# Down projection of a MoE's expert blocks: three rounded products of high and low parts in place of one full-precision product

## The chip, the cores and the metric

The kernel runs on one core of a Trainium2 chip. The time is device microseconds (us) of one execution; a result is the median of several runs. The profile is of one execution, with its own time beside it. Engine names: PE is TensorE, ACT is ScalarE, DVE is VectorE, POOL is GpSimd, SP is SyncE, which here only issues transfers.

## The reference, cut to what matters

One layer of a diffusion backbone: a mixer (mLSTM and RG-LRU), then a mixture of experts over 1152 tokens of width 1024 (64 experts of width 256, eight per token, one shared expert), then a final norm. The change touches one product, the last one of `expert_block`:

```
def expert_block(args):
    tok, e = args
    xb = x2d[tok]                                  # 128 gathered tokens x 1024
    hb = jax.nn.silu(xb @ exp_w1[e]) * (xb @ exp_w3[e])   # 128 x 256
    return hb @ exp_w2[e]                          # 256 -> 1024
yb = lax.map(expert_block, (slot_tok.reshape(NB, MOE_BLOCK), block_expert))
routed = segment_sum(yb.reshape(P, D) * slot_w[:, None], slot_tok, num_segments=N)
```

All arithmetic of the reference is float32.

## The kernel before, in words

The stages run one after the other, a barrier between them: norm, RG-LRU, mLSTM, routing, experts, final norm. The change is wholly in `stage_experts` (line 1350). Routing leaves a list of blocks of 128 token slots, each of one expert; the shared expert is taken as expert 64 with nine blocks at the end of the list. In this execution there are 114 blocks. Each engine has its own loop over pairs of blocks (Fori, two blocks in an iteration); the order of work on an engine is written out by hand and is fixed, and engines meet only through counting semaphores. An instruction that waits holds up all that is behind it on its engine.

What each engine does for block b, in the order of its loop:

- PE (lines 1574 to 1579): `turn_h(b)` transposes the 128x256 hidden tile (two transposes); `up(b+1)` computes both up projections of the next block; `turn(b+2)` transposes the gathered tokens of the block after (eight transposes); `down(b)` is the down projection: two halves of 512 columns, two steps of 128 along the inner width, four float32 matmuls, each of which the trace shows as two PE records. `up` already works as the change makes `down` work: its two operands are kept as a high part, rounded to the format fp32r, and a low part, the rest, and high*high + high*low + low*high is summed, 24 matmuls a block.
- ACT (lines 1622 to 1628): `ht(b)` copies the transposed hidden tile to SBUF; `high(b+2)` writes the rounded high part of the up weights, two instructions of 128x2048; `silu(b+1)`; `xt(b+2)` copies the transposed tokens, rounding them, two instructions; `y_half(b)` copies the result of `down(b)` from PSUM, two instructions (lines 1603 and 1604), after waiting that `down(b)` is done and that POOL has raised `scatter_done` for this buffer.
- DVE (lines 1667 to 1671): `low(b+2)` subtracts the high part from the up weights, two instructions of 128x2048 with both inputs in SBUF; `hidden(b+1)` multiplies silu, gate and slot weight; `x_low(b+2)` subtracts the high part of the tokens, two instructions that read PSUM.
- POOL (lines 1518 to 1521): `gather(b+4)` copies an index column and issues the gather of 128 rows; `scatter(b)` waits until the scatter before has landed (line 1503 then raises `scatter_done`), copies an index column, waits for `y_half(b)`, and issues a scatter that adds 128 rows of 1024 to the result in DRAM.
- SP (lines 1464 to 1469): the weights of an expert are three transfers of 1 MB in three slots: `issue_up` (lines 1414 and 1415) waits until the last block of the expert three before has its low part, `issue_down` (line 1424) waits for `down_done` of such a block.

Buffers: tokens, up-weight parts and y have two each; the PSUM tile of `down` and the transposed hidden tile have one.

Of the kernel before, what the change touches and what calls it, by code (L numbers as in the profile page):

```python
# [10 lines left out]
F32 = mybir.dt.float32  # L11
BF16 = mybir.dt.bfloat16
F32R = mybir.dt.float32r
# [1336 lines left out]
def stage_experts(nc, a, m):  # L1350

    with ExitStack() as ctx:
# [7 lines left out]
        wup = [[sb(f"wup{part}{j}", [P, 2, KT, DE], F32R) for part in "hl"] for j in range(2)]  # L1360
        idx_g, idx_s = [sb(f"idx_g{j}", [P, 1], I32) for j in range(2)], sb("idx_s", [P, 1], I32)
        hs, hb = [sb(f"hs{j}", [P, DE]) for j in range(2)], [sb(f"hb{j}", [P, DE]) for j in range(2)]
        hT = sb("hT5", [P, 2, P])
        y = [sb(f"y{j}", [P, D]) for j in range(2)]
        b_turn, b_up, b_h, b_down = m.banks[1:3], m.banks[3:5], m.banks[5], m.banks[6:8]
        s_w, s_w2 = [sem(f"ld_w{j}") for j in range(WSLOT)], [sem(f"ld_w2_{j}") for j in range(WSLOT)]
# [6 lines left out]
        w1 = a["exp_w1"][0].rearrange("e (p k) n -> e p k n", k=KT)  # L1373
        w3 = a["exp_w3"][0].rearrange("e (p k) n -> e p k n", k=KT)
        wd = a["exp_w2"][0].rearrange("e (p j) n -> e p j n", j=2)
        w_high, w_low, xt_low = (sem(n) for n in ("w_high", "w_low", "xT_low"))
        HALVES = [slice(0, 1), slice(1, 2)]
        block = ctx.enter_context(nc.Block())

# [5 lines left out]
        def pairs(eng):  # L1385
            return eng.value_load(m.tab[0:1, 4 * P + NE:4 * P + NE + 1], min_val=1, max_val=TABLE // 2)
# [7 lines left out]
        def expert(eng, b):  # L1394

            return entry(eng, bass.ds(b, 1), NE)
# [5 lines left out]
        @block.sync  # L1402
        def _(sp):
            def up_weights(e, r=None):

                slot = e % WSLOT
                if r is not None:
                    x = bass.ds(r * WSLOT + e, 1)
                    p1, p3 = (w[x].rearrange("e p k n -> (e p) k n") for w in (w1, w3))
                elif e < NE:  # L1410
                    p1, p3 = w1[e], w3[e]
                else:
                    p1, p3 = (a[n][0].rearrange("(p k) n -> p k n", k=KT) for n in ("shared_w1", "shared_w3"))
                sp.dma_start(w13[:, slot, 0, :, :], p1).then_inc(s_w[slot], 16)
                sp.dma_start(w13[:, slot, 1, :, :], p3).then_inc(s_w[slot], 16)

            def down_weights(e, r=None):
                if r is not None:
                    p2 = wd[bass.ds(r * WSLOT + e, 1)].rearrange("e p j n -> (e p) j n")
                elif e < NE:  # L1420
                    p2 = wd[e]
                else:
                    p2 = a["shared_w2"][0].rearrange("(p j) n -> p j n", j=2)
                sp.dma_start(w2[:, e % WSLOT, :, :], p2).then_inc(s_w2[e % WSLOT], 16)

            def ends(e, r=None):

                at = 4 * P + e
                return entry(sp, slice(at, at + 1) if r is None else bass.ds(r * WSLOT + at, 1), TABLE, 1)

            def issue_up(e, r=None):

                sp.wait_ge(w_low, 2 * ends(e - WSLOT, r))
                up_weights(e, r)

            def issue_down(e, r=None):

                sp.wait_ge(down_done, ends(e - WSLOT, r))
                down_weights(e, r)

            def up_landed(e, n):
                sp.wait_ge(s_w[e % WSLOT], 32 * n)
                sp.sem_inc(w_ready, 1)  # L1443

            def down_landed(e, n):
                sp.wait_ge(s_w2[e % WSLOT], 16 * n)
                sp.sem_inc(w2_ready, 1)

            up_weights(0)
            for e in range(1, WSLOT):  # L1450
                up_weights(e)
                down_weights(e - 1)
            down_weights(WSLOT - 1)
            up_landed(0, 1)
            down_landed(0, 1)
            up_landed(1, 1)
            for e in range(WSLOT, 2 * WSLOT):
                issue_up(e)
                up_landed(e - 1, (e - 1) // WSLOT + 1)
                if e > WSLOT:  # L1460
                    issue_down(e - 1)
                down_landed(e - 2, (e - 2) // WSLOT + 1)
            FULL = NE // WSLOT
            with sp.Fori(2, FULL) as r:
                for e in range(WSLOT):
                    issue_up(e, r)
                    up_landed(e - 1, r + (1 if e >= 1 else 0))
                    issue_down(e - 1, r)
                    down_landed(e - 2, r + (1 if e >= 2 else 0))
            for e in range(FULL * WSLOT, NX):  # L1470
                issue_up(e)
                up_landed(e - 1, (e - 1) // WSLOT + 1)
                issue_down(e - 1)
                down_landed(e - 2, (e - 2) // WSLOT + 1)
            up_landed(NE, NE // WSLOT + 1)
            issue_down(NE)
            for e in range(NE - 1, NX):
                down_landed(e, e // WSLOT + 1)
# [48 lines left out]
        def _(pe):  # L1527
# [25 lines left out]
                    mm = pe.transpose(b_h[:, i * P:(i + 1) * P], hb[j][:, i:DE:2], m.ident)  # L1553
                mm.then_inc(ht_out, 1)

            def down(b, j):
                e = expert(pe, b)
                slot = e % WSLOT
                pe.wait_ge(w2_ready, e + 1)
                pe.wait_ge(ht_ready, b + 1)  # L1560
                pe.wait_ge(y_act, b + 1)
                for half in range(2):
                    for i in range(2):
                        mm = pe.matmul(b_down[half][:, :], hT[:, i, :],  # L1564
                                       w2[:, bass.ds(slot, 1), i, half * 512:(half + 1) * 512].rearrange("p s n -> p (s n)"),
                                       start=(i == 0), stop=(i == 1))
                mm.then_inc(down_done, 1)

            n = pairs(pe)
# [4 lines left out]
            with pe.Fori(0, n) as r:  # L1574
                for u in range(2):
                    turn_h(r * 2 + u, u)
                    up(r * 2 + (u + 1), 1 - u)
                    turn(r * 2 + (u + 2), u)
                    down(r * 2 + u, u)

        @block.scalar
        def _(act):
# [12 lines left out]

            def ht(b):
                act.wait_ge(ht_out, b + 2)
                act.activation(hT[:, :, :], b_h[:, 0:DE].rearrange("p (i n) -> p i n", i=2), ACT.Copy).then_inc(ht_ready, 1)

            def y_half(b, j):  # L1600
                act.wait_ge(down_done, b + 1)
# [4 lines left out]
            def high(b, j):  # L1606
# [5 lines left out]
                for half in HALVES:  # L1612
                    act.activation(part13(wup[j][0], half), raw13(e % WSLOT, half), ACT.Copy).then_inc(w_high, 1)  # L1613

            n = pairs(act)
            act.sem_inc(y_act, 1)
            high(0, 0)
# [1 line left out]
            xt(1, 1)  # L1619
            high(1, 1)  # L1620
            silu(0, 0)
            with act.Fori(0, n) as r:
                for u in range(2):
                    ht(r * 2 + u)
                    high(r * 2 + (u + 2), u)
                    silu(r * 2 + (u + 1), 1 - u)
                    xt(r * 2 + (u + 2), u)
                    y_half(r * 2 + u, u)

        @block.vector  # L1630
        def _(dve):
            def hidden(b, j):
                dve.wait_ge(act_done, b + 1)
                if not (isinstance(b, int) and b < 2):
                    dve.wait_ge(ht_out, b)
                weight = m.slots[:, bass.ds(column(dve, b), 1), 1:2].rearrange("p c w -> p (c w)").bitcast(F32)
                dve.scalar_tensor_tensor(hb[j][:, :], hs[j][:, :], weight, b_up[j][:, DE:2 * DE], ALU.mult, ALU.mult).then_inc(h_done, 1)

            def low(b, j):

                e = expert(dve, b)
                dve.wait_ge(w_ready, e + 1)
                if not (isinstance(b, int) and b < 2):
                    dve.wait_ge(up_done, b - 1)
                for i, half in enumerate(HALVES):
                    dve.wait_ge(w_high, 2 * b + (i + 1))
                    dve.tensor_tensor(part13(wup[j][1], half), raw13(e % WSLOT, half),  # L1647
                                      part13(wup[j][0], half).bitcast(F32), ALU.subtract).then_inc(w_low, 1)

            def x_low(b, j):  # L1650

                dve.wait_ge(xt_ready, b + 1)
                if not (isinstance(b, int) and b < 2):
                    dve.wait_ge(up_done, b - 1)
                for i in range(2):
                    ins = dve.tensor_tensor(xT[j][1][:, 4 * i:4 * i + 4, :], b_turn[i][:, :].rearrange("p (k n) -> p k n", k=4),  # L1656
                                            xT[j][0][:, 4 * i:4 * i + 4, :].bitcast(F32), ALU.subtract)
                ins.then_inc(xt_low, 1)

            dve.sem_inc(h_done, 1)  # L1660
            low(0, 0)
            x_low(0, 0)
            x_low(1, 1)
            low(1, 1)
            hidden(0, 0)
            n = pairs(dve)
            with dve.Fori(0, n) as r:
                for u in range(2):
                    low(r * 2 + (u + 2), u)
                    hidden(r * 2 + (u + 1), 1 - u)  # L1670
                    x_low(r * 2 + (u + 2), u)


def stage_final(nc, a, o, m):
# [133 lines left out]
```

## Time and profile before

| | us |
|---|---|
| median of 3 runs | 2596.17 (2587.87 to 2598.42) |
| profiled execution, its own time | 2599.9 |
| its span in the trace | 2598.1 |
| start of the first y copy of `y_half` (block 0) | 1287.3 |
| start of the last one (block 113) | 2503.3 |

The span of the trace is the time from its first to its last instruction; the execution's own time has 1.8 us around it. The expert stage is read by its y copies: one per block, 113 intervals in 1216.0 us.

### The profile page before, as it was taken

What the parts mean: (1) busy time and instruction counts of PE and PEld (TensorE: products, weight loads), DVE (VectorE), ACT (ScalarE), POOL (GpSimd) and SP (SyncE); (2) the same over time, 40 slices, a digit from 0 to 9 for tenths busy, and PEclk for the clock granted to TensorE, in tenths of its full rate; (3) what the DMA queues carried; (4) which work ended last, traced back from release to release, by engine and by line L of the source; (5) the groups of instructions that cost most, each with busy time, mean ns of one, the idle gap of its engine ahead of it and who ended that gap; (6) DMA issues with size and microseconds to landing.
All of it is one profiled execution on the core that took longest, in us unless ns stands there. A gap on an engine that the chain in (4) does not pass through costs nothing. (4 is left out here: it accounts for less than half of the span.)

```text
span 2598.1 us, 30671 instructions
## 1 busy us (share of the span) xinstructions
PE 2072.1 (80%) x8111; PEld 1365.7 (53%) x8112; DVE 1290.0 (50%) x2151; ACT 1015.9 (39%) x1496; POOL 689.1 (27%) x616
## 2 busy tenths in 40 slices
PE   5587477499976785992599999999999989999950
PEld 0143233254866673541376666666766666666730
DVE  1334534500044554787365555556555555555547
ACT  1133434300011221110366555556665555555631
POOL 3010000000000000255134444444443444445430
PEclk9798687799977887995799999999999999999985
DMA  9741000021010004420797898976788899997554
GB/s 281 229 146 35 1 16 0 10 64 33 17 25 1 1 1 150 179 82 25 272 337 198 282 317 259 303 234 177 231 256 281 268 301 298 310 286 237 111 148 170
DMA packets 118319, 426.57 MB, mean 164 GB/s; under 512 B 22396, under 2 KB 36732, under 8 KB 93308
## 3 DMA queue, kind: packets, MB, share of 16 engines
q1 hardware_dynamic: 71372, 279.86, 29.4%
q0 software_dynamic: 46512, 145.97, 22.9%
q8 instruction: 27, 0.44, 0.1%
q14 instruction: 24, 0.20, 0.0%
q10 hardware_dynamic: 384, 0.11, 0.0%
HBM read 340.79 MB, written 85.67 MB: 164 GB/s over the span
## 5 line engine op out<-in xcount | busy, mean ns | idle before, releaser
L1647 DVE TENSOR_TENSOR wupl<-w,wuph 128x2048 fp32r<-128x2048 f32 x232 | 521.5, 2289 | 546.9 <-ACT wuph L1613 539.8
L1613 ACT ACTIVATE wuph<-w 128x2048 fp32r x232 | 432.3, 1918 | 38.3 <-SPq L1443 37.2
L1564 PE MATMUL bank<-w,hT 128*128 x912 | 415.7, 599 | 2.0 <-issue 1.7
L1546 PE MATMUL bank<-wuph,xTh 128*128 128x512 f32 x920 | 370.2, 402 | 17.7 <-DVE xTl L1656 17.7
L1546 PE MATMUL bank<-wuph,xTl 128*128 128x512 f32 x920 | 361.9, 393 | 0.0
L1546 PE MATMUL bank<-wupl,xTh 128*128 128x512 f32 x920 | 361.0, 392 | 0.0
L1564 PEld LDWEIGHTS bank<-w,hT 128*128 128x128 f32 x912 | 165.4, 191 | 172.3 <-issue 171.9
L1498 POOL DMA_INDIRECT xg<-hn_scratch,idx_g x118 | 211.2, 1790 | 96.3 <-POOL idx_g L1490 93.4
L1506 POOL DMA_INDIRECT yacc_scratch<-y,idx_s x114 | 184.1, 1615 | 115.6 <-ACT y L1604 65.7
L1603 ACT ACTIVATE y<-bank 128x512 f32<-128x512 f32 x114 | 68.2, 598 | 360.9 <-POOLq L1503 198.5
L1546 PEld LDWEIGHTS bank<-wuph,xTh 128*128 128x128 f32 x920 | 174.7, 190 | 55.6 <-issue 21.7
L1546 PEld LDWEIGHTS bank<-wuph,xTl 128*128 128x128 f32 x920 | 173.5, 189 | 37.1
L1546 PEld LDWEIGHTS bank<-wupl,xTh 128*128 128x128 f32 x920 | 174.1, 189 | 33.7
L1533 PE MATMUL bank<-cst,xg 128*128 128x128 f32 x928 | 127.8, 282 | 72.6 <-DMA xg<-hn_scratch,idx_g 69.9
L1490 POOL COPY idx_g<-shared 128x1 int32 x118 | 166.9, 1414 | 50.4 <-PE bank L1533 34.8
L1490 POOL COPY idx_s<-shared 128x1 int32 x114 | 51.5, 452 | 450.9 <-DMA yacc_scratch<-y,idx_s 444.3
L1533 PEld LDWEIGHTS bank<-cst,xg 128*128 128x128 f32 x928 | 121.1, 193 | 92.6 <-DMA xg<-hn_scratch,idx_g 85.7
L1656 DVE TENSOR_TENSOR xTl<-bank,xTh 128x512 fp32r<-128x512 f32 x232 | 148.8, 683 | 16.1 <-ACT xTh L1588 16.0
L864 PE MATMUL bank<-hnT,wg 128*128 128x512 f32 (+1 forms) x384 | 128.2, 497 | 33.1 <-DMA wg<-in_w_in 32.2
L1157 PE MATMUL bank<-wo,yT 128*128 128x512 f32 x288 | 130.2, 612 | 14.5 <-DMA wo<-in_w_out 14.5
L485 PE MATMUL bank<-hnT,wg 128*128 128x512 f32 (+1 forms) x384 | 131.6, 507 | 12.3 <-DMA bd<-in_rg_wx 12.2
L993 DVE SCALAR_TENSOR_TENSOR eb<-bank,cols,cst 128x128 f32<-128x128 f32 x72 | 20.3, 345 | 228.7 <-PE bank L898 228.4
(311 smaller groups left out, 2489.1 us busy)
## 6 DMA issues: line engine op xcount, KB each, us to landing
w<-in_exp_w SPq DMA_DIRECT2D x192, 1024.0 KB
wada<-in_w_ada SPq DMA_DIRECT2D x12, 2048.0 KB, 21.4
wg<-in_w_in SPq DMA_DIRECT2D x12, 1024.0 KB, 5.5
x<-x_scratch SPq DMA_DIRECT2D x18, 512.0 KB, 4.2
yacc_scratch<-zero POOLq DMA_DIRECT2D x10, 512.0 KB, 9.2
x_scratch<-x SPq DMA_DIRECT2D x9, 512.0 KB, 2.6
hn_scratch<-hn SPq DMA_DIRECT2D x9, 512.0 KB
y<-yacc_scratch SPq DMA_DIRECT2D x9, 512.0 KB, 4.6
```

The lines of the kernel that those rows point to most:

```text
L485: mm = pe.matmul(bank[:, 0:nt], wg[g % NWG][:, k, c0:c0 + P], m.hnT[:, k, t0:t0 + nt], start=(k == 0), stop=(k == KT - 1))
L864: mm = pe.matmul(bank[:, 0:nt], wg[g % NW][:, k, (mt % 2) * P:(mt % 2 + 1) * P], m.hnT[:, k, t0:t0 + nt], start=(k == 0), stop=(k == KT - 1))
L1157: mm = pe.matmul(bank[:, :], m.yT[:, k, t * P:(t + 1) * P], wo[:, k, half * 512:(half + 1) * 512], start=(k == 0), stop=(k == KT - 1))
L1490: pool.tensor_copy(dst[:, :], m.slots[:, bass.ds(c, 1), 0:1].rearrange("p c w -> p (c w)")).then_inc(listed, 1)
L1498: pool.indirect_dma_start(xg[j][:, :], None, m.hn2, bass.IndirectOffsetOnAxis(ap=idx_g[j][:, :], axis=0)).then_inc(gathered[j], 16)
L1506: pool.indirect_dma_start(m.yacc, bass.IndirectOffsetOnAxis(ap=idx_s[:, :], axis=0), y[j][:, :], None, compute_op=ALU.add).then_inc(scatte ...
L1533: mm = pe.transpose(b_turn[k // 4][:, (k % 4) * P:(k % 4 + 1) * P], xg[j][:, k:D:KT], m.ident)
L1546: mm = pe.matmul(b_up[j][:, :], x[:, k, :], w[:, :, k, :], start=(k == 0 and i == 0), stop=(k == KT - 1 and i == 2))
L1564: mm = pe.matmul(b_down[half][:, :], hT[:, i, :], w2[:, bass.ds(slot, 1), i, half * 512:(half + 1) * 512].rearrange("p s n -> p (s n)"), s ...
L1613: act.activation(part13(wup[j][0], half), raw13(e % WSLOT, half), ACT.Copy).then_inc(w_high, 1)
L1647: dve.tensor_tensor(part13(wup[j][1], half), raw13(e % WSLOT, half), part13(wup[j][0], half).bitcast(F32), ALU.subtract).then_inc(w_low, 1)
L1656: ins = dve.tensor_tensor(xT[j][1][:, 4 * i:4 * i + 4, :], b_turn[i][:, :].rearrange("p (k n) -> p k n", k=4), xT[j][0][:, 4 * i:4 * i + 4 ...
```

## The change

The inner product of `down` becomes three fp32r matmuls for each of the four float32 ones. For that `down_high` (ACT) writes the high part of the 128x2048 down weights of the block, `down_low` (DVE) the low part, `ht` writes the high part of the hidden tile in place of a plain copy, and `h_low` (DVE) its low part. The parts of the down weights, `wdn`, have one buffer, written anew for each block: `down_high(b+1)` waits for `down_done` of block b. `issue_down` on SP now waits for `wd_low`. In `hidden` the read of the column register stands ahead of the waits.

```
-        hT = sb("hT5", [P, 2, P])
+        hT = [sb(f"hT5{part}", [P, 2, P], F32R) for part in "hl"]
+        wdn = [sb(f"wdn{part}", [P, 2, D], F32R) for part in "hl"]
...
             def issue_down(e, r=None):
-                sp.wait_ge(down_done, ends(e - WSLOT, r))
+                sp.wait_ge(wd_low, ends(e - WSLOT, r))
...
-            def down(b, j):
-                e = expert(pe, b)
-                slot = e % WSLOT
-                pe.wait_ge(w2_ready, e + 1)
-                pe.wait_ge(ht_ready, b + 1)
+            def down(b):
+                pe.wait_ge(wd_low, b + 1)
+                pe.wait_ge(ht_low, b + 1)
                 pe.wait_ge(y_act, b + 1)
+                (hh, hl), (wh, wl) = hT, wdn
                 for half in range(2):
+                    c = slice(half * 512, (half + 1) * 512)
                     for i in range(2):
-                        mm = pe.matmul(b_down[half][:, :], hT[:, i, :],
-                                       w2[:, bass.ds(slot, 1), i, half * 512:(half + 1) * 512].rearrange("p s n -> p (s n)"),
-                                       start=(i == 0), stop=(i == 1))
+                        for q, (x, w) in enumerate(((hh, wh), (hh, wl), (hl, wh))):
+                            mm = pe.matmul(b_down[half][:, :], x[:, i, :], w[:, i, c], start=(i == 0 and q == 0), stop=(i == 1 and q == 2))
...
+            def down_high(b):                                  # ACT
+                e = expert(act, b)
+                act.wait_ge(w2_ready, e + 1)
+                if not (isinstance(b, int) and b == 0):
+                    act.wait_ge(down_done, b)
+                raw = w2[:, bass.ds(e % WSLOT, 1), :, :].rearrange("p s j n -> p (s j) n")
+                act.activation(wdn[0][:, :, :], raw, ACT.Copy).then_inc(wd_high, 1)
...
                     ht(r * 2 + u)
                     high(r * 2 + (u + 2), u)
                     silu(r * 2 + (u + 1), 1 - u)
                     xt(r * 2 + (u + 2), u)
+                    down_high(r * 2 + (u + 1))
                     y_half(r * 2 + u, u)
...
+            def down_low(b):                                   # DVE
+                e = expert(dve, b)
+                dve.wait_ge(wd_high, b + 1)
+                raw = w2[:, bass.ds(e % WSLOT, 1), :, :].rearrange("p s j n -> p (s j) n")
+                dve.tensor_tensor(wdn[1][:, :, :], raw, wdn[0][:, :, :].bitcast(F32), ALU.subtract).then_inc(wd_low, 1)
+            def h_low(b):
+                dve.wait_ge(ht_ready, b + 1)
+                dve.tensor_tensor(hT[1][:, :, :], b_h[:, 0:DE].rearrange("p (i n) -> p i n", i=2),
+                                  hT[0][:, :, :].bitcast(F32), ALU.subtract).then_inc(ht_low, 1)
...
                 for u in range(2):
+                    h_low(r * 2 + u)
                     low(r * 2 + (u + 2), u)
                     hidden(r * 2 + (u + 1), 1 - u)
                     x_low(r * 2 + (u + 2), u)
+                    down_low(r * 2 + (u + 1))
```

Ahead of the loops, ACT does `down_high(0)` after `silu(0)` and DVE `down_low(0)` after `hidden(0)`.

## Rows read from the trace of the kernel before

**Rows 1.** The page, busy time of each engine, its share of the span, instructions.
```profile
PE 2072.1 (80%) x8111; PEld 1365.7 (53%) x8112; DVE 1290.0 (50%) x2151; ACT 1015.9 (39%) x1496; POOL 689.1 (27%) x616
```

**Rows 2.** Line 1603: duration in ns (min, median, max), first and last start.
```profile
L1603 ACT ACTIVATE y<-bank x114: 597/598/601, 1287.3 to 2503.3; 128x512 f32<-128x512 f32 x114
```

**Rows 3.** Windows of the stage: blocks 0 to 6, 7 to 104, 105 to 112.
```profile
core 0: us, PE busy (x) PEld busy (x) DVE busy (x) ACT busy (x) POOL busy (x), PEclk, DMA share, GB/s
1287.30:1357.60 70.30, 70.30 (x296) 50.07 (x296) 42.59 (x35) 45.07 (x56) 23.20 (x24) 1.00 0.94 311
1357.60:2422.90 1065.30, 1013.93 (x4120) 705.24 (x4118) 598.50 (x490) 626.66 (x784) 489.06 (x394) 1.00 0.84 263
2422.90:2503.30 80.40, 80.40 (x336) 56.92 (x335) 48.68 (x40) 51.50 (x64) 38.82 (x34) 1.00 0.48 104
```

**Rows 4.** Waits, 1300 to 2500: total us, times, longest.
```profile
POOL idx_s L1490 <- DMA yacc_scratch<-y,idx_s: 441.0, 93, 9.2
ACT y L1603 <- POOLq L1503: 198.5, 46, 6.9
PE bank L1546 <- DVE xTl L1656: 17.7, 23, 0.9
```

**Rows 5.** Timeline of PE, one block: start, us, instruction.
```profile
1977.71 0.48 PE L1546 MATMUL bank<-wuph,xTh 128*128 128x512 f32 x1
...
1983.05 0.40 PE L1546 MATMUL bank<-wuph,xTl 128*128 128x512 f32 x1
1983.28 1.05 PE L1533 MATMUL bank<-cst,xg 128*128 128x128 f32 x8
1984.17 3.60 PE L1564 MATMUL bank<-w,hT 128*128 x8
1987.61 0.39 PE L1553 MATMUL bank<-cst,hb 128*128 128x128 f32 x2
```

**Rows 6.** Timeline of ACT over the same block.
```profile
1977.76 0.60 ACT L1603 ACTIVATE y<-bank 128x512 f32<-128x512 f32 x1 [2.35 <-PE bank L1564]
...
1978.73 0.39 ACT L1598 ACTIVATE hT<-bank 128x256 f32<-128x256 f32 x1
1979.00 3.73 ACT L1613 ACTIVATE wuph<-w 128x2048 fp32r x2
```

**Rows 7.** Timeline of DVE over the same block.
```profile
1981.13 4.49 DVE L1647 TENSOR_TENSOR wupl<-w,wuph 128x2048 fp32r<-128x2048 f32 x2 [3.96 <-ACT wuph L1613]
1985.55 0.47 DVE L1637 SCALAR_TENSOR_TENSOR hb<-hs,shared,bank 128x256 f32<-128x256 f32 x1
1985.94 1.28 DVE L1656 TENSOR_TENSOR xTl<-bank,xTh 128x512 fp32r<-128x512 f32 x2
```

**Rows 8.** The page, costliest groups: busy us, mean ns, idle before.
```profile
L1647 DVE TENSOR_TENSOR wupl<-w,wuph 128x2048 fp32r<-128x2048 f32 x232 | 521.5, 2289 | 546.9 <-ACT wuph L1613 539.8
L1613 ACT ACTIVATE wuph<-w 128x2048 fp32r x232 | 432.3, 1918 | 38.3 <-SPq L1443 37.2
```

**Rows 9.** Timeline of POOL, two scatters and what follows them.
```profile
1968.18 1.59 POOL L1506 DMA_INDIRECT yacc_scratch<-y,idx_s  x1 [0.91 <-POOL idx_s L1490]
...
1975.48 0.18 POOL L1490 COPY idx_s<-shared 128x1 int32 x1 [3.69 <-DMA yacc_scratch<-y,idx_s]
1976.66 1.59 POOL L1506 DMA_INDIRECT yacc_scratch<-y,idx_s  x1 [1.00 <-POOL idx_s L1490]
...
1988.37 0.18 POOL L1490 COPY idx_s<-shared 128x1 int32 x1 [8.11 <-DMA yacc_scratch<-y,idx_s]
```

**Rows 10.** Timeline of SP in that window: weight transfers issued.
```profile
1975.76 0.34 SPq L1414 DMA_DIRECT2D w<-in_exp_w  x1
...
1977.95 0.01 SPq L1424 DMA_DIRECT2D w<-in_exp_w  x1
```

**Rows 11.** Timelines of DVE and POOL, a scatter issued during a subtraction.
```profile
1320.82 4.49 DVE L1647 TENSOR_TENSOR wupl<-w,wuph 128x2048 fp32r<-128x2048 f32 x2 [3.96 <-ACT wuph L1613]
...
1321.57 3.01 POOL L1506 DMA_INDIRECT yacc_scratch<-y,idx_s  x1 [0.91 <-POOL idx_s L1490]
```

More of the change, by code:

```diff
@@ L1375, in stage_experts @@
         wd = a["exp_w2"][0].rearrange("e (p j) n -> e p j n", j=2)
-        w_high, w_low, xt_low = (sem(n) for n in ("w_high", "w_low", "xT_low"))
+        w_high, w_low, xt_low, wd_high, wd_low, ht_low = (sem(n) for n in (
+            "w_high", "w_low", "xT_low", "wd_high", "wd_low", "hT_low"))
         HALVES = [slice(0, 1), slice(1, 2)]
@@ L1578, in _ @@
                     turn(r * 2 + (u + 2), u)
-                    down(r * 2 + u, u)
+                    down(r * 2 + u)
         @block.scalar
@@ L1597, in ht @@
                 act.wait_ge(ht_out, b + 2)
-                act.activation(hT[:, :, :], b_h[:, 0:DE].rearrange("p (i n) -> p i n", i=2), ACT.Copy).then_inc(ht_ready, 1)
+                act.activation(hT[0][:, :, :], b_h[:, 0:DE].rearrange("p (i n) -> p i n", i=2), ACT.Copy).then_inc(ht_ready, 1)
             def y_half(b, j):
@@ L1621, in _ @@
             silu(0, 0)
+            down_high(0)
             with act.Fori(0, n) as r:
@@ L1632, in hidden @@
             def hidden(b, j):
+                weight = m.slots[:, bass.ds(column(dve, b), 1), 1:2].rearrange("p c w -> p (c w)").bitcast(F32)
                 dve.wait_ge(act_done, b + 1)
@@ L1635, in hidden @@
                     dve.wait_ge(ht_out, b)
-                weight = m.slots[:, bass.ds(column(dve, b), 1), 1:2].rearrange("p c w -> p (c w)").bitcast(F32)
                 dve.scalar_tensor_tensor(hb[j][:, :], hs[j][:, :], weight, b_up[j][:, DE:2 * DE], ALU.mult, ALU.mult).then_inc(h_done, 1)
@@ L1665, in _ @@
             hidden(0, 0)
+            down_low(0)
             n = pairs(dve)
```

## The prediction

> **What bounds the kernel now.** I read the page's busy shares first: PE is busy for 80% of the span, no other engine for more than 50% [rows 1]. That invites the reading "PE is the limit, so cheaper matmuls are time won", and the next views are there to test it. The line of the y copies gives the pace of the stage: 114 copies from 1287.3 to 2503.3, 113 intervals in 1216.0 us, 10.76 us a block [rows 2]. The windows split that in three. In the first 7 and the last 8 intervals PE is busy without a gap, 70.30 of 70.30 and 80.40 of 80.40 us, so a block takes 10.04 and 10.05 us and PE sets the pace. The 98 in between take 1065.3 us, 10.87 each, at the full granted clock (1.00, that is 2.4 GHz), so the lost 0.8 us is no matter of the clock [rows 3]. Counted in the timeline of the same copies (114 of them, the first and last as in [rows 2]), 41 of the 113 intervals are 10.05 within 0.03 and the other 72 average 11.17.
>
> The table of waits says what those 72 wait for. POOL waits in 93 blocks for the scatter before to land, 441.0 us in all, and in 46 blocks the y copy waits for POOL's signal after that landing, 198.5 us; PE's own waits for DVE are small, 17.7 us in 23 blocks [rows 4]. One scatter is out at a time, and its landing is short or long: issued at 1968.18 it was down by 1975.48, 7.3 us; issued at 1976.66, with weight transfers issued at 1975.76 and 1977.95 around it, it was down at 1988.37, 11.7 us [rows 9, 10]. The next one follows 1.18 us after the index copy begins [rows 9], so a loop is about 8.5 or 12.9 us. So two limits share the stage: PE in the clean blocks, the scatter loop with one y buffer of slack in the others.
>
> **PE: what the change gives.** `down` takes from 1984.17 to 1987.61, 3.44 us, for eight records [rows 5]. The first and last of the 24 up matmuls start at 1977.71 and 1983.05, so one fp32r matmul of 512 columns costs 5.34 / 23 = 0.232 us, and the 24 with what lies around them 5.57. Twelve cost 2.75 with this step; the new `down` is 0.7 us shorter. PE's own work in a block falls from 10.05 to 9.35 us. If PE alone set the pace of all blocks, that would be 0.7 x 114 = 80 us.
>
> **ACT and DVE: what it adds.** `down_high` is the shape of `high`, 1.92 us to its end and about 1.82 to the next start (3.73 for two, overlapping by 0.1) [rows 6, 8]. `down_low` is the shape of `low`, 2.29 us to its end, 2.2 to the next start [rows 7, 8]. `h_low` reads 128x256 from PSUM; it isn't in the trace. Nearest rows: `hidden`, the same size, 0.47, and one of the two `x_low` instructions of twice the size, 0.68 (two in 1.28) [rows 7]. I take 0.4, between zero and 0.68. Per block ACT's work goes from some 6.7 to 8.6 us and DVE's from 6.1 to 8.8. Both sums are under 9.35, so by sums alone nothing new binds. The order is what matters.
>
> **The chain through the order.** `down_high(b+1)` can't start before `down(b)` ends, since `wdn` has one buffer, and it is ahead of `y_half(b)`, `ht(b+1)` and `high(b+3)` on ACT. Follow it from the start of `up(b+2)`:
>
> - up 5.57, turn 0.89, down to its end 2.9 (2.75 and 0.16 for the last record's end) [rows 5]: 9.36
> - to ACT 0.04, `down_high` 1.82, `y_half` 0.97 (1977.76 to 1978.73), `ht` 0.27, first half of `high` 1.92 [rows 6, 8]: 5.02
> - to DVE 0.21 (1979.00 + 1.92 against 1981.13), two `low` 4.42, `hidden` 0.39, `x_low` 1.28 [rows 6, 7]: 6.30, and 0.06 back to PE: `up(b+4)` starts.
>
> Sum 20.7 us for two blocks, 10.37 a block. The same walk in the kernel before has no `down_high` and the longer `down`: 20.7 - 1.82 + 0.7 = 19.6, or 9.8 a block, under PE's 10.05. That is checked by the row: `x_low` ends at 1987.22 and PE starts the next `up` some 0.5 us later, after `turn_h`, without having waited [rows 5, 7]. The chain was hidden by 0.25 us a block, and the change adds 1.1 us to its two blocks. So a clean block goes from 10.05 to about 10.36, and PE waits about 1 us in each for `x_low`. The new instructions on DVE fit beside: with the end of `down(b)` as zero, `down_low(b+1)` runs from 2.1 to 4.4, `h_low(b+1)` to 4.8, and `low(b+3)` may start at 5.2. `down(b+1)` starts at some 7, so it waits for neither. If `low` were held up by them, each us would be half a us a block.
>
> Clean blocks: 41 x 0.31 = 13 us lost.
>
> **The other 72 blocks.** If the scatter's landing sets their pace and lands as before, they lose nothing; if they carry the longer chain on top, they lose 0.31 as the clean ones do; and POOL meets a new obstacle. A scatter issued while DVE subtracts weights took 3.01 instead of 1.59 us: it began at 1321.57, 0.75 us into the subtraction that began at 1320.82 [rows 11]. Such subtractions fill 4.5 us of a block now, and 6.8 after. The third one comes just where `y_half(b)` ends and the scatter of b is due (zero is again the end of `down`: y done at 3.0, `down_low` to 4.4). At random, two POOL instructions of a loop (index copy and scatter) would each meet 2.29 of 10.9 us, 21%, and lose half of it, 1.1 us: 0.5 us a block; it is zero if they fall in the gaps. So 72 blocks cost between 0 and 0.8 us each; I take 0.25, nearer to the small end because the loop has a buffer of slack: 18 us.
>
> The Trainium skill has the rule for this (SBUF — State Buffer, "SBUF: two separate sides"): the port pair that VectorE and GpSimd share is an exclusive lock, held for the whole instruction, and a VectorE instruction with two SBUF inputs can hold it against GpSimd. This trace agrees, with 3.01 against 1.59 us. By the rule `h_low` and `x_low`, with one input in PSUM, block nothing, and `down_low` does in every block; taken for every scatter, with 1.1 us each on the loop, 72 blocks would lose 80 us in place of the 18.
>
> **Other edits.** SP asks for the down weights after `wd_low` in place of `down_done`, earlier by about a block. No weight is late now (it isn't among the waits of ACT's `high`: idle 38.3 us in all, 37.2 of it the first load [rows 8]), so that earns nothing. Reading the column register ahead of the waits in `hidden`: `hidden` follows `low` without a gap now [rows 7], nothing. Ahead of the loop `down_high(0)` and `down_low(0)` put up to 2 us in front of block 0, and at the end the last scatter comes at most 2 us later. I put 2 for both.
>
> **Sum.** 13 + 18 + 2 = 33 us on the profiled execution's own 2599.9: 2633. The median of the runs is 3.7 us lower, so 2629; I say 2627, rounding down as part of 18 is uncertain.
>
> **Rivals.**
>
> - *PE stays the limit, the time falls.* It needs the chain of two blocks to be under 2 x 9.35 = 18.7 us in place of 20.7; it decides there. For it: PE's share of 80% and gapless PE in 15 blocks. Against it: each term of the chain is a row, and the chain was within 0.25 us of PE before. If it held, 41 clean blocks would win 0.7 each and the others from nothing to 0.7: 29 to 80 us, so some 2515 to 2567. It could also come in part by shorter landings in the 72 blocks. 10%.
> - *The landing sets the middle of the stage and the clean blocks are a smaller part than counted:* only the 13 us of the clean blocks, or less where landings get a bit shorter. 2596 + 8, within half a per cent. For it: 93 waits for landing [rows 4]. 20%.
> - *The weights burst.* Now up weights are asked for at the end of `low` and down weights 2.2 us later (1975.76 and 1977.95) [rows 10]. After, the wait of `issue_down` is already met when SP reaches it, so 3 MB go out together just ahead of a scatter. If 15 to 20 more of the 113 scatters take the long landing, 4.4 us more (11.7 against 7.3), that is 65 to 90 us on top: about 2700. Against it: the bytes are the same and the scatter next to it would go free. 12%.
>
> My forecast itself has 58%: the chain at 10.36 in clean blocks, some loss in the others, 2612 to 2655.
>
> **How the numbers follow.** What this measurement can tell from no change is 0.5%, 13 us. Faster by more than that: the first rival, 0.10. Within: the second and a little of the forecast's low end, 0.21. Slower: the rest, 0.69. Range 2592 to 2682: below it the faster rival, above it the full burst; it holds the bounds 0 and 0.8 us for the 72 blocks up to 80% of the upper one.
>
> **What would show it.** In the first and last window of the stage: y copies 10.3 to 10.5 us apart, PE no longer busy without a gap, and its wait there for `x_low` (xTl) in nearly every block, about 1 us. `down` at 2.7 us for twelve records. ACT: `down_high` directly after the last matmul of `down`, then y. POOL: more scatters or index copies of over 2 us. Wrong if clean blocks take 9.4 us; wrong in size if the middle of the stage stays at 10.87 or goes beyond 11.4.

## The result, and the profile after

The changed kernel takes 2660.43 us (median of 4 runs, 2653.79 to 2670.77) against 2592.02 of the kernel before: 1.0265 times, 95% interval 1.0243 to 1.0288. The forecast was 2627. The profiled execution took 2670.77 with a span of 2668.7, 70.6 us more than the span of before.

First the busy shares of the page and the line of the y copies, then the windows of the stage, cut and with columns as in [rows 3] (blocks 0 to 6, 7 to 104, 105 to 112):

```profile
PE 2044.5 (77%) x8567; PEld 1472.5 (55%) x8567; DVE 1594.2 (60%) x2380; ACT 1219.1 (46%) x1611; POOL 848.1 (32%) x616
```
```profile
L1604 ACT ACTIVATE y<-bank x114: 574/580/602, 1285.2 to 2578.2; 128x512 f32<-128x512 f32 x114
```
```profile
1285.20:1359.50 74.30, 67.23 (x315) 54.78 (x313) 61.04 (x49) 56.81 (x64) 36.29 (x23) 0.98 0.85 278
1359.50:2490.50 1131.00, 991.27 (x4517) 798.52 (x4518) 858.11 (x687) 800.75 (x884) 628.42 (x396) 0.97 0.79 248
2490.50:2578.20 87.70, 78.07 (x359) 63.43 (x357) 70.06 (x56) 65.02 (x74) 47.09 (x34) 0.96 0.48 102
```

PE is busy for 27.6 us less in the whole span, and the stage is 77 us longer. The first window grew from 70.3 to 74.3, the last from 80.4 to 87.7, the middle from 1065.3 to 1131.0, 0.67 us a block. So 66 of the 77 us are in the middle; the rest of the kernel gave 6.4 back (y copies start 2.1 us earlier, and 4.3 less after the last). PE, gapless in the outer windows before, now is busy for 67.23 of 74.30 and 78.07 of 87.70 us, and the granted clock, 1.00 in all three before, is 0.96 to 0.98.

The waits, 1300 to 2580, answering to [rows 4]:

```profile
POOL idx_s L1492 <- DMA yacc_scratch<-y,idx_s: 360.0, 97, 8.3
PE bank L1535 <- DMA xg<-hn_scratch,idx_g: 47.2, 31, 3.9
PE bank L1555 <- DVE hb L1649: 44.8, 48, 1.6
DVE wdnl L1677 <- ACT wdnh L1623: 163.3, 105, 4.6
PE bank L1548 <- DVE xTl L1668: 59.1, 70, 0.9
ACT y L1604 <- POOLq L1505: 56.8, 34, 5.1
```

PE waits for the low part of the tokens in 70 blocks (23 before) and for the hidden tile in 48 (3 before); for gathered tokens, whose gathers stand behind the scatters in POOL's order, it waits 47.2 us (28.6 before). POOL waits less for landings (360 against 441 us) though its loop is longer, so it loses time somewhere else. Where, the page's groups say: mean ns of one, then idle before and its releaser.

```profile
L1508 POOL DMA_INDIRECT yacc_scratch<-y,idx_s x114 | 266.8, 2340 | 117.3 <-POOL idx_s L1492 80.7
L1492 POOL COPY idx_s<-shared 128x1 int32 x114 | 89.9, 789 | 366.9 <-DMA yacc_scratch<-y,idx_s 362.2
```

A scatter instruction takes 2.34 us on average, where before most took 1.59 [rows 9]; the index copy 0.79, where its shortest is 0.18.

Of the outer windows the timeline shows the form. One pair of blocks, ACT, then DVE, then PE, all up to the second `up`:

```profile
2532.52 1.92 ACT L1623 ACTIVATE wdnh<-w 128x2048 fp32r x1 [1.86 <-PE bank L1567]
2534.34 0.58 ACT L1604 ACTIVATE y<-bank 128x512 f32<-128x512 f32 x1
...
2535.30 0.38 ACT L1599 ACTIVATE hT5h<-bank 128x256 fp32r<-128x256 f32 x1
2535.56 3.73 ACT L1614 ACTIVATE wuph<-w 128x2048 fp32r x2
```
```profile
2534.65 2.29 DVE L1677 TENSOR_TENSOR wdnl<-w,wdnh 128x2048 fp32r<-128x2048 f32 x1 [2.66 <-ACT wdnh L1623]
2536.86 0.42 DVE L1682 TENSOR_TENSOR hT5l<-bank,hT5h 128x256 fp32r<-128x256 f32 x1
2537.70 4.50 DVE L1659 TENSOR_TENSOR wupl<-w,wuph 128x2048 fp32r<-128x2048 f32 x2 [0.42 <-ACT wuph L1614]
...
2542.51 1.28 DVE L1668 TENSOR_TENSOR xTl<-bank,xTh 128x512 fp32r<-128x512 f32 x2
```
```profile
2531.89 0.40 PE L1567 MATMUL bank<-wdnh,hT5l 128*128 128x512 f32 x1
...
2542.64 0.51 PE L1555 MATMUL bank<-cst,hb 128*128 128x128 f32 x2 [1.01 <-DVE hb L1649]
2544.04 0.47 PE L1548 MATMUL bank<-wuph,xTh 128*128 128x512 f32 x1 [0.89 <-DVE xTl L1668]
```

`down` ends at 2532.29; from there `down_high`, y copy, `ht`, first half of `high`, `low`, `hidden`, `x_low`, and PE starts `up` at 2544.04 after two gaps. The next pair does the same 21.13 us later (the next `up` with both gaps is at 2565.17). In the last blocks y copies alternate at 9.33 and 11.8 us: PE runs free in one block and waits in the next.

### The profile page after: what moved, and what is told of

Read it like the earlier page. It is cut to its first block and busy times, and to the rows that moved or that the text cites. A ratio compares the mean times of both kernels' runs of the same rounds, so it can differ in the third digit from the quotient of the medians.

```text
span 2668.7 us, 32220 instructions
## 1 busy us (share of the span) xinstructions
PE 2044.5 (77%) x8567; PEld 1472.5 (55%) x8567; DVE 1594.2 (60%) x2380; ACT 1219.1 (46%) x1611; POOL 848.1 (32%) x616
## 5 line engine op out<-in xcount | busy, mean ns | idle before, releaser
L1548 PE MATMUL bank<-wuph,xTh 128*128 128x512 f32 x920 | 382.5, 416 | 61.1 <-DVE xTl L1668 60.0
L1677 DVE TENSOR_TENSOR wdnl<-w,wdnh 128x2048 fp32r<-128x2048 f32 x115 | 263.7, 2293 | 167.8 <-ACT wdnh L1623 167.5
L1623 ACT ACTIVATE wdnh<-w 128x2048 fp32r x115 | 220.1, 1914 | 197.2 <-PE bank L1567 191.3
L1508 POOL DMA_INDIRECT yacc_scratch<-y,idx_s x114 | 266.8, 2340 | 117.3 <-POOL idx_s L1492 80.7
L1500 POOL DMA_INDIRECT xg<-hn_scratch,idx_g x118 | 229.6, 1946 | 96.3 <-POOL idx_g L1492 93.4
L1492 POOL COPY idx_s<-shared 128x1 int32 x114 | 89.9, 789 | 366.9 <-DMA yacc_scratch<-y,idx_s 362.2
L1492 POOL COPY idx_g<-shared 128x1 int32 x118 | 189.7, 1608 | 47.5 <-PE bank L1535 25.4
L1567 PE MATMUL bank<-wdnh,hT5h 128*128 128x512 f32 x456 | 191.0, 419 | 0.0
L1567 PE MATMUL bank<-wdnh,hT5l 128*128 128x512 f32 x456 | 181.8, 399 | 0.0
L1567 PE MATMUL bank<-wdnl,hT5h 128*128 128x512 f32 x456 | 181.2, 397 | 0.0
L1668 DVE TENSOR_TENSOR xTl<-bank,xTh 128x512 fp32r<-128x512 f32 x232 | 148.9, 684 | 29.8 <-ACT xTh L1589 28.6
## 6 DMA issues: line engine op xcount, KB each, us to landing
wada<-in_w_ada SPq DMA_DIRECT2D x12, 2048.0 KB, 21.1
```

The lines of the kernel that those rows point to most:

```text
L1492: pool.tensor_copy(dst[:, :], m.slots[:, bass.ds(c, 1), 0:1].rearrange("p c w -> p (c w)")).then_inc(listed, 1)
L1500: pool.indirect_dma_start(xg[j][:, :], None, m.hn2, bass.IndirectOffsetOnAxis(ap=idx_g[j][:, :], axis=0)).then_inc(gathered[j], 16)
L1508: pool.indirect_dma_start(m.yacc, bass.IndirectOffsetOnAxis(ap=idx_s[:, :], axis=0), y[j][:, :], None, compute_op=ALU.add).then_inc(scatte ...
L1548: mm = pe.matmul(b_up[j][:, :], x[:, k, :], w[:, :, k, :], start=(k == 0 and i == 0), stop=(k == KT - 1 and i == 2))
L1567: mm = pe.matmul(b_down[half][:, :], x[:, i, :], w[:, i, c], start=(i == 0 and q == 0), stop=(i == 1 and q == 2))
L1623: act.activation(wdn[0][:, :, :], raw, ACT.Copy).then_inc(wd_high, 1)
```

## The experiments

The table is from the POOL timeline of each profile: from the 7th to the 106th scatter, so the middle 99 intervals, the mean of the scatter instruction, from its end to the next index copy (the landing), the copy, the gap after it, and their sum. "Long up" counts, in the loop without its first blocks, the `up`s whose 24 matmuls start over more than 5.8 us (5.33 is the rule). The last eight blocks are in us per block. Each ratio is to runs of the kernel before in the same series (medians 2588.4 to 2594.7, here 2592.0), and costs of different series are compared by it. In e8 to e12 the index copy stands elsewhere in the loop; they have no row.

| kernel | us | ratio to before | scatter | landing | copy | gap | loop | last 8 blocks | long up |
|---|---|---|---|---|---|---|---|---|---|
| before | 2592.0 | 1 | 1.59 | 7.92 | 0.35 | 0.99 | 10.84 | 10.05 | 1 |
| changed | 2660.4 | 1.0265 | 2.25 | 7.44 | 0.79 | 0.99 | 11.48 | 10.96 | 18 |
| e1 parts once | 2570.2 | 0.9942 | 1.62 | 7.82 | 0.29 | 0.99 | 10.72 | 9.85 | 12 |
| e2 no down_high | 2602.0 | 1.0050 | 2.10 | 7.51 | 0.42 | 0.99 | 11.02 | 9.93 | 10 |
| e3 no down_low | 2601.7 | 1.0059 | 1.85 | 7.69 | 0.46 | 0.99 | 10.99 | 10.55 | 15 |
| e4 filler | 2650.1 | 1.0251 | 2.24 | 7.47 | 0.68 | 0.99 | 11.38 | 10.54 | 1 |
| e5 SP wait | 2656.0 | 1.0262 | 2.27 | 7.33 | 0.77 | 0.99 | 11.35 | 10.55 | 17 |
| e6 pieces | 2628.2 | 1.0136 | 1.83 | 7.91 | 0.38 | 0.99 | 11.10 | 10.95 | 17 |
| e7 halves | 2592.0 | 1.0004 | 1.73 | 7.71 | 0.44 | 0.99 | 10.86 | 10.14 | 5 |

**e1, the gain without its price.** The parts of the down weights are written for block 0 only, and used for all.

```
-                sp.wait_ge(wd_low, ends(e - WSLOT, r))
+                sp.wait_ge(down_done, ends(e - WSLOT, r))
-                pe.wait_ge(wd_low, b + 1)
+                pe.wait_ge(wd_low, 1)
-                    down_high(r * 2 + (u + 1))        # ACT's loop
-                    down_low(r * 2 + (u + 1))         # DVE's loop
```

> The changed kernel without down_high and down_low in the loop: the parts of the down weights are written once, for block 0, and used for every block; SP waits for down_done again. PE's three fp32r products per float32 one and h_low stay. It is the gain on PE without its price on ACT and DVE. Theory (chain through down_high, then the scatter loop): first and last blocks at PE's own 9.35 us, granted clock back at 1.00, the 98 blocks in between held by the scatter loop, so faster than before by 30 to 60 us only: 2535 to 2565. Rival (PE alone sets the pace): all blocks gain 0.7 us, 80 us, 2512. Rival (the new matmuls themselves are slow or the fp32r format costs something): no faster than before, 2590.

Measured: 2570.2 us, 0.9942 (0.9923 to 0.9962), a gain of 18 us where PE saves 80. That rejects both rivals (2512, and no gain), and the theory's 2535 to 2565 was too good as well. The middle took 10.75 us a block, 0.12 less than before: the scatter loop, not PE. But the outer blocks took 9.74 and 9.85, not 9.35: the old chain of ACT and DVE, hidden at 10.05, came out. In the last eight blocks y copies come at 9.35 and 10.0 to 11.0 in turn, PE with the same wait for `x_low`, 40.9 us in 52 blocks. The granted clock wasn't back, as had been expected: 12 long `up`s.

```profile
PE bank L1548 <- DVE xTl L1667: 40.9, 52, 0.9
ACT y L1604 <- POOLq L1505: 238.7, 69, 7.0
```

**e2 and e3, one half of the price each.** e2 takes `down_high` out of ACT's loop, and `down_low` waits for the weights and `down_done` itself:

```
-                    down_high(r * 2 + (u + 1))
-                dve.wait_ge(wd_high, b + 1)
+                dve.wait_ge(wd_high, 1)
+                dve.wait_ge(w2_ready, e + 1)
+                if not (isinstance(b, int) and b == 0):
+                    dve.wait_ge(down_done, b)
```

> The changed kernel without down_high in the loop (the high part of block 0's down weights stays); down_low on DVE stays in every block and waits for down_done and the weights itself. Theory (down_high on the two-block chain is the cost): 2.0 us leave the chain of 21.1, first and last blocks at 9.5 to 9.7 us, the clock back at 1.00 nearly everywhere, total 2570 to 2600. Rival (POOL held up by the third subtraction in each block is the cost): it is still there, so 2630 or more, and scatters of over 2 us stay as many.

e3 takes `down_low` out of DVE's loop; PE and SP wait for `wd_high` instead:

```
-                    down_low(r * 2 + (u + 1))
-                pe.wait_ge(wd_low, b + 1)
+                pe.wait_ge(wd_low, 1)
+                pe.wait_ge(wd_high, b + 1)
```

> The changed kernel without down_low in the loop (the low part of block 0's down weights stays); down_high on ACT stays, SP and PE wait for it. Theory: down_low isn't on the chain, so the first and last blocks stay at pairs of 21.1 us and the clock still falls at times; POOL is held up less, which gives 10 to 30 us: 2630 to 2650. Rival (lock of POOL or DVE's load is the main cost): back to 2600 or less, with scatters at 1.59 us.

Measured: e2 2602.0 us, 1.0050 (1.0030 to 1.0070), and e3 2601.7, 1.0059 (1.0036 to 1.0082). By the ratios either gives back some 55 us of 68. In the last eight blocks the chain theory holds in both: without `down_high` they take 9.93, above the 9.5 to 9.7 expected, without `down_low` 10.55, which is the clean pair of 21.1. In the first seven it doesn't show: they take 10.62 in both, as in the changed kernel (10.61). In e2 their intervals go from 8.1 to 13.7, and y copies wait 13.7 us there for POOL; so these blocks aren't limited by the chain alone. e2's total is just above what was expected (2570 to 2600), with 10 long `up`s where the clock was to be back nearly everywhere, and with 39 scatters of over 2 us against 54. For e3 the expectation failed: 10 to 30 us were to come, some 55 came, so what `down_low` does to POOL costs more than I had put. The page's line of the index copy shows it, e3 against 789 ns above:

```profile
L1492 POOL COPY idx_s<-shared 128x1 int32 x114 | 57.6, 505 | 490.1 <-DMA yacc_scratch<-y,idx_s 487.6
```

And the two aren't additive: the loop is 11.0 with one of them and 11.5 with both. A longer chain also moves y copies and subtractions against POOL's instructions; the count in the next part shows it.

**e4, PE kept at work.** Four transposes of the identity into an unused bank ahead of `turn_h` and four ahead of `up`.

```
+            def filler():
+                for _ in range(4):
+                    pe.transpose(m.banks[0][:, 0:P], m.ident, m.ident)
```

> The changed kernel with four transposes of the identity into an unused PSUM bank ahead of turn_h and four ahead of up in every block: work for PE in the gaps it has (2.4 us in a pair of blocks), 0.9 us a block. Theory (PE's gaps let the granted clock fall to half for some 3.4 us in 18 blocks, 1.5 us lost each): the long up's go, the pairs stay at 21.1 us, 20 to 27 us faster than the changed kernel, 2635. Rival (the falls of the clock don't come from the gaps, or the lost time is on no path): within 5 us of 2660. Rival (the filler is itself on the path): slower, up to 0.9 us a block, 2700 and more.

Measured: 2650.1 us, 1.0251 (1.0220 to 1.0282), by the times not told from the changed kernel. The 20 to 27 us that were expected did not come. By the profile the theory holds as far as the clock goes: one long `up` in the loop in place of 18, and the last eight blocks at 10.54, the pair of 21.1 without the 13.3s that the changed kernel has among them. The window of the last eight shows the clock back:

```profile
2468.90:2553.20 84.30, 80.90 (x419) 67.80 (x417) 69.69 (x56) 65.39 (x73) 43.86 (x33) 1.00 0.45 99
```

The stage is 13 us shorter, not the 29 that 18 long `up`s lose. Probably most of that falls, in the middle, into time in which the scatter is waited for anyway; no run shows it.

**e5, SP's wait.** One line: `issue_down` waits for `down_done` again.

> The changed kernel with issue_down on SP waiting for down_done again. Theory (the loop of one scatter at a time, lengthened by what POOL waits for DVE's subtractions, paces the middle blocks): where the down weights are asked for matters little, within 8 us of 2660. Rival (three transfers of an expert leave together just ahead of a scatter and make more landings long): 20 us faster or more, and fewer landings of over 8.4 us than the 37 in the middle 99 of the changed kernel.

Measured: 1.0262 (1.0229 to 1.0294), the same. Landings over 8.4 us from the end of the scatter instruction: 33 of 99 against 37, and 43 in the kernel before. The burst of three weight transfers is rejected as a cost of 20 us or more.

**e6, the same subtraction in four pieces.** This is the test of the hold itself: DVE has no less to do.

```
-                raw = w2[:, bass.ds(e % WSLOT, 1), :, :].rearrange("p s j n -> p (s j) n")
-                dve.tensor_tensor(wdn[1][:, :, :], raw, wdn[0][:, :, :].bitcast(F32), ALU.subtract).then_inc(wd_low, 1)
+                for i in range(4):
+                    c = slice(i * 256, (i + 1) * 256)
+                    raw = w2[:, bass.ds(e % WSLOT, 1), :, c].rearrange("p s j n -> p (s j) n")
+                    ins = dve.tensor_tensor(wdn[1][:, :, c], raw, wdn[0][:, :, c].bitcast(F32), ALU.subtract)
+                ins.then_inc(wd_low, 1)
```

> The changed kernel with down_low as four subtractions of 128x512 in place of one of 128x2048: the same work on DVE, some 0.3 us longer in all, but POOL can get in between them. Theory (POOL waits for the end of the one instruction): the mean scatter in the middle falls from 2.25 us toward 1.9, the index copy from 0.79 toward 0.6, the loop of 11.47 us by 0.3 to 0.5, total 20 to 45 us faster than 2660. Rival (it is DVE's load, or the chain, and not the hold on POOL): no faster, or slower by the added DVE time.

Measured: 2628.2 us, 1.0136 (1.0117 to 1.0154), 32 us faster with 22.6 us more on DVE in the stage (1011.81 against 989.21). Scatter and copy fell as expected:

```profile
L1508 POOL DMA_INDIRECT yacc_scratch<-y,idx_s x114 | 207.2, 1817 | 126.3 <-POOL idx_s L1492 65.1
L1492 POOL COPY idx_s<-shared 128x1 int32 x114 | 43.8, 384 | 438.3 <-DMA yacc_scratch<-y,idx_s 430.6
```

Half of it came back as longer landings, 7.91 against 7.44, so that the loop fell by 0.38. The rival (DVE's load) is rejected. But the edit also moved POOL's instructions against DVE's: of the 83 us that scatters and index copies lost, 51 are of those begun in `down_low` and 33 of those begun in `low` (counted in the next part), so this is not a test of the hold by `down_low` alone.

**e7, down in two column halves.** PE signals after the first half; `down_high` and `down_low` work on 128x(2x512) each.

```
-                if not (isinstance(b, int) and b == 0):
-                    act.wait_ge(down_done, b)
+                for half in range(2):
+                    c = slice(half * 512, (half + 1) * 512)
+                    if not (isinstance(b, int) and b == 0):
+                        act.wait_ge((down_half, down_done)[half], b)
...
-                pe.wait_ge(wd_low, b + 1)
+                    pe.wait_ge(wd_low, 2 * b + (half + 1))
...
-                mm.then_inc(down_done, 1)
+                    mm.then_inc((down_half, down_done)[half], 1)
```

> The changed kernel with down_high, down_low and the wait of PE for them split by the two column halves of down: the first half of down_high(b+1) starts when the first half of down(b) is done, 1.4 us earlier. Theory (chain): about 0.9 us leave the 21.1 of a pair, so the first and last blocks take 10.1 to 10.2 us in place of 10.56, and the middle, held by the scatter loop, moves by less than 0.3: 2630 to 2650. Rival (the last blocks are held by POOL too): they stay at 10.5.

Measured: 2592.0 us, 1.0004 (0.9987 to 1.0021): the whole loss is gone, more than expected (2630 to 2650). The last eight take 10.14, as expected, the first seven 10.48 and not 10.1 to 10.2; the middle was to move by less than 0.3 us a block and moved by 0.63. The edit does two things, a shorter chain and a shorter hold of POOL in one; e6 has only the shorter instructions and gave 32 of the 68 us. How the other 36 split between the chain and the timing of POOL's instructions isn't settled.

**e8 and e9, one scatter loop shorter.** The middle was said to be paced by the scatter loop. Then taking the index copy out of it must show, in both kernels. Two index buffers, copied before the wait for the landing:

```
+                tokens(b, idx_s[j], 2 * b + 6)
                 if not (isinstance(b, int) and b == 0):
                     hold(scattered, b * 16)
                     pool.sem_inc(scatter_done, 1)
-                tokens(b, idx_s, 2 * b + 6)
```

> The changed kernel with two index buffers for the scatter, so that POOL copies the index column before it waits for the landing of the scatter before: the copy and the gap behind it (0.79 and 0.99 us on average in the middle) leave the scatter loop. Theory (the middle 98 blocks are paced by that loop): the loop falls from 11.47 to some 10.6 to 10.9, where the chain at 10.56 begins to bind, 55 to 85 us faster: 2575 to 2605. Rival (the middle is paced by the ACT and DVE chain, the scatter just follows): under 15 us.

> The kernel before (float32 down) with the early index copy alone: two index buffers for the scatter, copied before the wait for the landing. Theory (before the change, too, the middle 98 blocks were paced by the scatter loop, 10.84 us there): the loop falls by about 1.2 us below PE's 10.05, so nearly all blocks come at 10.05 to 10.2, 60 to 80 us faster than before: 2510 to 2530. Rival (the index copy is at work in the shadow of something else): within 15 us of 2589.

Measured: e8, the changed kernel with it, 2596.2 us, 1.0018 (0.9999 to 1.0038), 64 us faster; e9, the kernel before with it, 2529.9 us, 0.9752 (0.9729 to 0.9775). e8's middle is 10.86 a block, which is what the chain of 10.56 gives with e8's 18 long `up`s there (18 x 1.6 / 98 = 0.29); e9's is 10.29. In e9's windows PE has hardly a gap left:

```profile
1350.20:2359.10 1008.90, 992.74 (x4120) 703.03 (x4119) 597.58 (x490) 629.75 (x785) 385.36 (x394) 1.00 0.88 278
2359.10:2439.40 80.30, 80.23 (x336) 56.86 (x334) 48.68 (x40) 51.47 (x65) 26.00 (x32) 1.00 0.50 104
```

So the scatter loop paced the middle of both. The rival (the scatter only follows) is rejected.

**e10 to e12, together.** e10 has halves and early copy; e11 also two subtractions per half; e12 also the y copies between the halves of `high`:

```
+                for i, half in enumerate(HALVES):
                     act.activation(part13(wup[j][0], half), raw13(e % WSLOT, half), ACT.Copy).then_inc(w_high, 1)
+                    if between is not None and i == 0:
+                        between()                      # y_half(b - 1)
```

> The changed kernel with both the split in column halves and the early index copy. Theory: the two limits are separate and both fall, the chain to 10.1 us a block and the scatter loop to about 10 to 10.4; the middle takes 10.2 to 10.5, the total is 2530 to 2560. Rival (one cost counted twice): no faster than the better of the two alone, 2590.

> As halves and early index copy together, with down_low in four subtractions of 128x512. Theory: POOL is held shorter, the loop falls by another 0.2 to 0.4 us where it still binds, 5 to 20 us faster than without the pieces. Rival: the loop no longer binds, no difference or some us slower by the added DVE time.

> As the one with the pieces, and on ACT the y copies of block b stand between the two halves of high(b+3) in place of ahead of ht(b+1). Theory (chain): the 0.97 us of y leave the way to the first half of high, the second half comes 0.5 us late for DVE, so 0.4 to 0.9 us leave a pair of 20.2: first and last blocks 9.7 to 9.9 us, 10 to 30 us faster than e11. Rival: y is now done 2.2 us later, the scatter and the next down wait for it, and the loop takes back what the chain gives: no difference or slower.

Measured: 2547.6 us, 0.9820 (0.9792 to 0.9848); 2541.8, 0.9801 (0.9770 to 0.9831); 2545.5, 0.9814 (0.9792 to 0.9836). The two limits are separate and both fall (e10: middle 10.43). The pieces can't be told from none here; 5 to 20 us were expected. e12 does shorten the chain, 9.87 a block in the first seven and in seven of the last eight (the very last interval, 8.06, has no next block behind it) against e11's 10.00 and 10.09, and loses it in the middle, 10.51 against 10.35, with 55 scatters of over 2 us against 29: the rival won. All three beat the kernel before and the changed one; none has a lower median than e9, which has no split at all (the intervals of e9 and e11 just overlap).

## Why the prediction was right in sign and short by half

The median of 2660 lies above the 2612 to 2655 that the prediction gave its own case; of the 35 us that it forecast, and the 68 that came, these are the terms.

- **What bounds the kernel** held for the kernel before: two limits share the stage, and the one that isn't PE is the scatter loop (e8, e9, the small gain of e1). After the change the chain takes PE's place beside it.
- **PE's gain** held. The first and last matmul of the new `down` stand 2.60 us apart (2529.29 to 2531.89), eleven steps of 0.24; from its start to the next transposes it takes 2.84 us in place of 3.44, and a block that waits for nothing 9.33 in place of 10.05.
- **The chain** held in its order and was short in size. Forecast 20.7 us for two blocks, measured 21.1. Two handovers were mis-sized: from the end of `down` to `down_high` 0.23 us, not 0.04 (2532.29 to 2532.52), and from `x_low` to `up` 0.25, not 0.06 (2543.79 to 2544.04). The wait has another form than forecast: not 1 us in each block for `x_low`, but 1.01 for `hidden` and 0.89 for `x_low` in every second one. e2 and e7 show that the chain through `down_high` sets the last blocks, e3 that `down_low` isn't on it.
- **The outer windows** lost 11 us of the 77; 15 blocks at 0.31 would be 5. Besides the 0.4 of a pair, blocks of 13.3 us came in that the forecast hadn't: the clock, below.
- **The other 72 blocks** is the step that failed in size: "I take 0.25, nearer to the small end because the loop has a buffer of slack". With the clean ones among them the middle was priced at 26 x 0.31 + 72 x 0.25 = 26 us, and lost 66. By the prediction's own sign, a middle beyond 11.4, it was wrong in size: 11.54. The random estimate of 0.5 us a loop was nearer: scatter and copy together grew by 1.10 us, landings gave 0.48 back. The buffer of slack doesn't take that up, since the loop itself is the limit. One scatter beside `down_low` shows the form, with the subtraction that it met, begun 0.59 us before it:

```profile
1870.63 3.17 POOL L1508 DMA_INDIRECT yacc_scratch<-y,idx_s  x1 [0.99 <-POOL idx_s L1492]
```
```profile
1870.04 2.29 DVE L1677 TENSOR_TENSOR wdnl<-w,wdnh 128x2048 fp32r<-128x2048 f32 x1 [1.34 <-ACT wdnh L1623]
```

  The scatter ends 1.47 us after the subtraction does. So do, within 1.46 to 1.51 us, all but two of the 18 scatters of the stage that begin in `down_low`; the two began within 0.04 us of its start and took 1.59. The 41 that begin in `low` end 3.75 to 3.78 or 5.95 to 5.97 us after its start, again some 1.47 us after the first or the second of its two subtractions. Every scatter that begins in neither takes 1.59.

  But `down_low` is only part of what POOL lost. Count, for the 99 intervals of the table, the time above 1.59 and 0.18 us of scatters and index copies, by the subtraction in which they begin:

| kernel | in `low`: scatters, copies | us above | in `down_low`: scatters, copies | us above |
|---|---|---|---|---|
| before | 0, 12 | 16 | | |
| changed | 26, 16 | 58 | 16, 35 | 69 |
| e3 | 20, 30 | 53 | | |
| e6 | 13, 14 | 24 | 39, 31 | 18 |
| e7 | 5, 10 | 15 | 22, 26 | 25 |

  The forecast's random estimate comes to 42 meetings with `down_low` of 1.1 us each; there were 51 of 1.35. What it put at nothing is that the new timing also moves POOL's instructions into `low`, where no scatter of these intervals began before: 41 us more. In e6 `down_low` is met 70 times in place of 51 and costs a quarter.

  The Trainium skill's rule (SBUF — State Buffer, "SBUF: two separate sides") says that the shared port pair is locked for the whole instruction, and the traces agree: a scatter ends a fixed 1.5 us after the subtraction, and shorter subtractions hold it for less (e6). Taken for every scatter the rule gave 80 us for the 72 blocks, and with the 26 clean ones 88 for the middle, above the 66 measured.
- **The rivals.** PE as the limit is rejected by e1. The landing alone, within half a per cent, is rejected by the time. The weights burst, which was to cost 65 to 90 us, is rejected by e5.
- **SP's wait** was put at nothing, and is, within the noise of e5. The earlier read of the column register, put at nothing too, has no run of its own.
- **The 2 us** ahead of the loop and behind it did not show: outside the stage the profile is 6.4 us shorter. No run separates that; the first y copy comes anywhere from 1269.6 to 1287.3 us in the profiles.

## What to carry to other kernels

A stage can have a second limit whose engine looks idle: POOL was busy for 32% and its loop of copy, issue and landing was full. Add up such a loop from issue to issue before pricing anything else. A longer part of it comes back in every block, though not whole: here landings shortened by about half of what the other parts grew by (0.48 of 1.10 us, and 0.47 of 0.83 the other way in e6). When work is put on another engine, ask what it holds while it runs, and what it moves into the way of other instructions, not only how long it takes: with the same subtraction in four pieces the change cost half as much. And an operand made per block in a single buffer puts its maker between the end of one product and all that follows; splitting it so that it starts at the half gave back the whole loss here, by that and by shorter instructions together.

## What the runs showed of the hardware that wasn't expected

The granted clock of PE fell in a stage in which PE is busy 88% of the time (1136.58 of 1293 us). After the gaps of 1.01 and 0.89 us before 2565.17, `up` began at full pace, then went to matmuls 0.43 us apart in place of 0.23 for three microseconds; the windows give 0.72 and 0.59 of the clock, where the lower level is 1.2 GHz of 2.4.

```profile
2565.17 0.47 PE L1548 MATMUL bank<-wuph,xTh 128*128 128x512 f32 x1 [0.89 <-DVE xTl L1668]
...
2567.04 0.63 PE L1548 MATMUL bank<-wuph,xTh 128*128 128x512 f32 x1
2567.47 0.63 PE L1548 MATMUL bank<-wupl,xTh 128*128 128x512 f32 x1
```
```profile
2565.00:2567.50 2.50, 2.33 (x8) 1.89 (x9) 2.39 (x2) 2.50 (x4) 0.19 (x1) 0.72 1.00 243
2567.50:2570.00 2.50, 2.50 (x8) 2.00 (x7) 2.08 (x2) 2.25 (x2) 1.14 (x2) 0.59 0.16 64
```

It made `up` 1.6 us longer in 17 of 114 blocks and 2.8 in one; the same two gaps before 2544.04 had no such fall behind them. With 0.9 us of filler a block it came once (e4), as in the kernel before, whose clean blocks have no gaps. Why it came 18 times and not in every pair of blocks isn't settled.
